# A hybrid short-convolution and Conformer decoder step: the way of the GLU output, the carried history and the convolution weights through DRAM, and the order of requests in the head

## The chip, the cores and the metric

The kernel runs on the 8 cores of one Trainium2 chip. Each core handles one prompt sequence of 2048 tokens and 16 sampling sequences of 8 new tokens each (128 sample rows), and the cores do not talk to each other. The time is the device time, in microseconds (us), of the slowest core.

## The reference, cut to what matters

```python
u = rmsnorm(h, g_mix)
a_b, a_c, a_h, a_z, b_v, b_g, b_z, gate_a, gate_b = split(u @ w_in)   # nine columns of 1024
# branch A: short gated convolution, 3 taps
s  = a_c * a_h
ya = (a_b * dwconv(concat(buf_a, s), w_conv_a) * silu(a_z)) @ w_out_a
# branch B: GLU, depthwise convolution with 31 taps, layer norm
v  = b_v * sigmoid(b_g)
ext_b = concat(buf_b, v)            # 30 carried rows (zeros for the prompt), then the new ones
c  = dwconv(ext_b, w_conv_b) + b_conv_b
yb = (silu(layernorm(c)) * silu(b_z)) @ w_out_b
new_buf_b = ext_b[:, -30:]          # sample: 22 old rows and the 8 new ones
# merge, embedding, last norm
h = h + (sigmoid(gate_a) * ya + sigmoid(gate_b) * yb) @ w_o
h = h + sigmoid(rmsnorm(h, g_ple) @ w_pg) * (p @ w_pe)
return rmsnorm(h, g_final), new_buf_a, new_buf_b
```

All matrices are 1024 wide. Inputs and weights lie in DRAM as float32; the kernel multiplies in bf16.

## The kernel before

The 2048 prompt tokens are done in two blocks of 1024; block 1 also takes the 128 sample rows (`ns = 128`, T = 1152). Each block goes through these stages, in each of which j counts eight chunks of 128 channels:

- **Head** (block 0 only, `head()`, L1029): eight tiles of x (512 KB each, issued by SyncE at L458 and L462) are squared and summed on ScalarE (`stats`, L374), the factor is made on GpSimd (L383, L388), VectorE scales (L1037), TensorE turns the tile (L1044), VectorE writes it into `uT` (L1047), and TensorE begins the first three weight columns in pieces of 128 tokens (`part`).
- **Stage B**, the loop over j at L1091: `s3_chunk(j)` (four units: h, c, z, b of branch A), `conv(j)` (the 31 taps of branch B for chunk j), `glu(j + 2)` (two units, gate and value), `wcv_load(j + 2)`. In block 1 `conv_s(j)`, the same convolution for the sample rows, is put in the middle of `glu(j + 2)`. So the GLU output of chunk j is made one whole `s3_chunk`, one `conv`, one `glu` and one more `s3_chunk` before `conv(j)` wants it.
- **Stages C and D** (L1108 to L1133): the z of branch B, the norm, output matrices of both branches, gates. **Stage E** (L1141 to L1195): 128-token tiles through w_o, w_pg and w_pe to the output, and in block 0 also the norm and the turn of block 1's x. It keeps three helpers of interest: `A_turn_dma` turns a tile by a transposing DMA, `A_turn_pe` by TensorE (tile 0 only), `palloc` gives out pairs of PSUM banks.

A **unit** (`unit_u`, L533) is one 128-column slice of weights against all T tokens: 16 matmuls of 128x512 in block 0, and 8 of 128x128 more in block 1. All are recorded at L525. Weights come from DRAM through a ring of 14 buffers: `pump` (L342) puts the next requests on GpSimd's queue, each waiting for TensorE to be done with the buffer it overwrites.

`conv(j)` needs 16 tokens by 2 channels on the partitions, so `glu_evac` (L564) sends v through DRAM. VectorE writes v into `vt[v]` as [128 channels][16 phases][W] (L570); SyncE writes it to `vd` (L597), in 2048 runs of W bf16 numbers; three loads on SyncE's queue fetch it as three 32-partition bands of `R` (L601), each waiting for that write. W is 66 in block 0 (2 + 64). In block 1 it is 114, because the sample history rides along: for each chunk `sample_hist` (L552) loads 128 x 16 x 48 float32 numbers of `sb` into columns 66 to 113 of `vt` (L555) and doubles them on GpSimd (L557), and VectorE puts the eight new rows between them (L577). `sample_hist(j + 2)` stands at the end of `glu_evac(j)`, and its multiply waits for its load on GpSimd's queue.

The weights of the convolution, `w_cv`, are 96 x 2048 float32 numbers for each chunk, of which every second one is zero: the two channels of a pair share partitions, so each has zeros where the other has its weights. `wcv_load` (L560) puts the load on GpSimd's queue.

Each engine works strictly in the order of the program (`Sched.emit`), and waits at an instruction until all its releasers have come. DMA queues of one engine are issued in that order too: at L601 SyncE waits for the write of L597, and the next chunk's L597 stands behind it. In the head `pump(2)`, `pump(1, after=["x3"])` and `pump(NRING, after=["x7"])` (L470 to L472) stand ahead of the statistics on GpSimd's queue.

Of the kernel before, what the change touches and what calls it, by code (L numbers as in the profile page):

```python
# [156 lines left out]
def build_program():  # L157
# [11 lines left out]
    sb_d = din("sb", [D, NPH, 48])  # L169
# [4 lines left out]
    w_cv = din("w_cv", [NCH, 96, 2 * D])  # L174
# [13 lines left out]
    vd = [nc.dram_tensor(f"vd{i}", [NCH, NPH, 128, b["W"]], BF16).ap() for i, b in enumerate(BLOCKS)]  # L188
    st_d = [nc.dram_tensor(f"st{i}", [2, NP + b["ns"]], F32).ap() for i, b in enumerate(BLOCKS)]

    with contextlib.ExitStack() as st:
# [53 lines left out]
        for k in range(NCH):  # L245
# [5 lines left out]

        RB = NCOL * WMAX * 2
        WR = Region("wr", 2 * RB + 2 * 4096)
        R = [WR.at(RB * i, RB // 2, BF16, [f"R{i}_{s}" for s in range(3)], group=f"R{i}") for i in range(2)]
        wcv = [WR.at(2 * RB + 4096 * i, 2 * D, BF16, [f"wcv{i}"]) for i in range(2)]
# [6 lines left out]
        u2T = [TA.at(2048 * i, D, BF16, [f"u2T{i}"]).rearrange("p (k t) -> p k t", k=NCH) for i in range(2)]  # L262
# [10 lines left out]
        VB = NPH * WMAX * 2  # L273
        XV = Region("xv", 2 * SX * 4 + 2 * VB)
        sext = [XV.at(SX * 4 * i, SX, F32, [f"sext{i}{q}" for q in ("", "l", "h", "g", "n")], group=f"sext{i}")
                for i in range(2)]
        vt = [XV.at(2 * SX * 4 + VB * i, VB // 2, BF16, [f"vt{i}{q}" for q in ("", "h", "s", "n")], group=f"vt{i}")
              for i in range(2)]
        NXS = 4
# [181 lines left out]
        for i in range(1, 8):  # L461
# [7 lines left out]
                                               scalar2=None, op0=ALU.mult), reads=["vecs"], writes=["vecs"])  # L469
        pump(2)  # L470
        pump(1, after=["x3"])
        pump(NRING, after=["x7"])  # L472
# [27 lines left out]
        def do_block(bi, blk):  # L500
            ns, W = blk["ns"], blk["W"]
# [50 lines left out]
            def sample_hist(j):  # L552
                v = j % 2
                dst = vt[v][:, 0:NPH * W].rearrange("p (h w) -> p h w", h=NPH)[:, :, 66:114]
                S.add("pool", lambda e: e.dma_start(out=dst, in_=sb_d[128 * j:128 * j + 128, :, :]),  # L555
                      writes=[f"vt{v}s", f"vt{v}n"], dma=f"vts{v}")
                S.add("pool", lambda e: e.tensor_scalar(out=dst, in0=dst, scalar1=2.0, scalar2=None, op0=ALU.mult),  # L557
                      reads=[f"vt{v}s"], writes=[f"vt{v}s"])

            def wcv_load(j):  # L560
                S.add("pool", lambda e: e.dma_start(out=wcv[j % 2][0:96, :], in_=w_cv[j, :, :]),
                      writes=[f"wcv{j % 2}"], dma=f"wcv{j % 2}")

            def glu_evac(j, bg_, bv):  # L564
# [8 lines left out]
                    reads=pres(bv) + [tgr], writes=[f"vt{v}"])  # L573
                vres = [f"vt{v}", f"vt{v}h"]
                if ns:
                    new = vv[:, 8:16, 66:114].rearrange("p t (q c) -> p t q c", c=3)[:, :, :, 2]
                    S.add("dve", lambda e: e.scalar_tensor_tensor(  # L577
                        out=new, in0=tg[:, NP:T].rearrange("p (t q) -> p t q", t=8), scalar=1.0,
                        in1=pf(bv, NP, T).rearrange("p (t q) -> p t q", t=8), op0=ALU.add, op1=ALU.mult),
                        reads=pres(bv) + [tgr, f"vt{v}s"], writes=[f"vt{v}n"])  # L580
                    vres += [f"vt{v}s", f"vt{v}n"]
# [12 lines left out]
                else:  # L594
                    S.add("act", lambda e: e.copy(out=halo_v[:, j, :, :], in_=vv[:, :, 64:66]),
                          reads=[f"vt{v}"], writes=[f"halo_v{j}"])
# [11 lines left out]
                if ns and j + 2 < NCH:  # L608
                    sample_hist(j + 2)
# [19 lines left out]
            def conv(j):  # L629
                v = j % 2  # L630
                rr = [f"R{v}_{s}" for s in range(3)] + [f"wcv{v}"]
# [88 lines left out]
            def s3_chunk(j, mid=None, mid2=None):  # L720
# [169 lines left out]
            pair_ctr = [3]  # L890
# [38 lines left out]
            def A_turn_dma(t):  # L929
                sl = t % 2  # L930
                S.add("sp", lambda e: e.dma_start_transpose(out=u2T[sl], in_=xb[sl]),
                      reads=[f"xb{sl}"], writes=[f"u2T{sl}"], dma=f"u2T{sl}")

            def A_turn_pe(t):
                sl = t % 2
                b = palloc()
                for k in range(NCH):
                    S.add("pe", lambda e, k=k: e.transpose(out=psb[:, b, k * 128:(k + 1) * 128],
                                                           in_=xb[sl][:, k * 128:(k + 1) * 128], identity=idb[:]),
                          reads=[f"xb{sl}", "idb"], writes=pr2(b))  # L940
                S.add("dve", lambda e: e.tensor_copy(out=u2T[sl], in_=psb[:, b, :].rearrange("p (k t) -> p k t", t=128)),
                      reads=pr2(b), writes=[f"u2T{sl}"])
# [205 lines left out]
            for t in range(nt):  # L1148
# [20 lines left out]
                if t > 0:  # L1169
                    D_out(t - 1)  # L1170
# [131 lines left out]
```

How the kernel before makes its waits and increments, by code:

```python
            def run(engname, e):  # L112
                waited = {}
                for o in ops:
                    if o["eng"] != engname:
                        continue
                    need = {}
                    for d in o["deps"]:
                        od = ops[d]
                        v = od["seq"] * (16 if od["dma"] is not None else 1)
                        if v > need.get(od["chan"], 0):
                            need[od["chan"]] = v
                    for c, v in need.items():
                        if waited.get(c, 0) >= v:
                            continue
                        e.wait_ge(sems[c], v)
                        waited[c] = v
                    ins = o["fn"](e)
                    if o["signal"]:
                        ins.then_inc(sems[o["chan"]], 16 if o["dma"] is not None else 1)
                if engname == final_wait_eng:
                    for c, v in final.items():
                        if waited.get(c, 0) < v:
                            e.wait_ge(sems[c], v)
```

## Time and profile before

| | |
|---|---|
| Time, median of 3 runs | 1092.92 us (1092.85 to 1106.76) |
| The profiled execution | 1104.08 us, span 1102.5 us on the slowest core |
| Spans of the 8 cores | 1078.5 to 1102.5 us |
| TensorE busy, matmuls | 848.4 us, 77% |
| VectorE, ScalarE, GpSimd busy | 468.9, 270.0 and 216.7 us |
| Stage B of block 0, first to last conv | 96.6 to 285.1 us |
| Stage B of block 1, first to last conv | 602.7 to 815.6 us |

Matmuls can overlap weight loads. An engine's busy time leaves out the instructions that issue DMAs, registers and semaphores. A row of the timeline has a start, a length, the engine (SPq is SyncE's queue), the line of the kernel, the operation, the tile written and read, and in brackets the idle time before it with what ended it.

### The profile page before, as it was taken

How to read it: one execution, taken by the hardware profiler on the slowest of the kernel's cores; microseconds unless marked ns; L12 is line 12 of the kernel's file. 1: busy time of each engine (PE TensorE's matmuls, PEld its weight loads, DVE VectorE, ACT ScalarE, POOL GpSimd, SP SyncE). 2: the span in 40 equal slices, each digit the busy share in tenths (PEclk: the TensorE clock that was granted, in tenths of full speed). 3: DMA queues.
4: the chain of work that ended last, by engine and by line, in shares of the span. 5: the costliest groups of instructions: out<-in, count | busy, mean ns of one | idle time of the engine just before them, and what ended most of it. 6: DMA issues, size and time to landing. Idle time of an engine off the chain costs nothing.

```text
span 1102.5 us, 15552 instructions; the slowest of 8 cores (1078.5 to 1102.5 us)
## 1 busy us (share of the span) xinstructions
PE 848.4 (77%) x5876; PEld 408.7 (37%) x5876; DVE 468.9 (43%) x469; ACT 270.0 (24%) x388; POOL 216.7 (20%) x362
## 2 busy tenths in 40 slices
PE   0664939598489899998851997798645989999993
PEld 0522414243234344433420543354322544454431
DVE  0511515445539322367310455364436572213554
ACT  3010202121125321356210112122102443112542
POOL 2210101011012121245213121305000222100231
PEclk9986969799789999999885999799967999999997
DMA  8598999989349675898798698999951986402632
GB/s 199 90 88 124 121 102 103 119 105 132 65 108 189 114 115 83 151 239 207 88 106 133 88 111 101 137 141 150 120 90 30 199 140 105 78 1 62 147 90 87
DMA packets 120419, 128.46 MB, mean 117 GB/s; under 512 B 80744, under 2 KB 82040, under 8 KB 118776
## 3 DMA queue, kind: packets, MB, share of 16 engines
q0 software_dynamic: 49520, 64.60, 45.6%
q1 hardware_dynamic: 70680, 62.59, 29.0%
q8 instruction: 48, 0.79, 0.3%
q14 instruction: 27, 0.22, 0.1%
q10 hardware_dynamic: 144, 0.26, 0.1%
HBM read 170.10 MB, written 17.06 MB: 170 GB/s over the span
## 4 chain that ended last, share of the span: by engine, by line
PE 41%; DMA 34%; DVE 11%; issue 7%; ACT 2%; POOL 2%; SPq 1%; DVEq 0%; POOLq 0%; ACTq 0%
PE ps L525 34%; DMA vd<-t_xv 18%; DMA t_xv<-sb 6%; PE ps L965 3%; DMA t_wr<-vd 3%; PE ps L909 2%; DMA t_wr<-w_cv 2%; DVE t_tmp L843 2%; DVE t_c L855 2%; DMA t_c<-x 1%; DVE t_tmp L991 1%; DVE t_tmp L999 1%; DMA t_wr<-w_pg 1%; PE ps L635 1%; DVE t_tmp L919 1%
## 5 line engine op out<-in xcount | busy, mean ns | idle before, releaser
L525 PE MATMUL ps<-t_uT,t_ring 128*128 128x512 bf16 (+1 forms) x2976 | 563.4, 351 | 18.1 <-DVE t_vkeep L588 12.3
L525 PEld LDWEIGHTS ps<-t_uT,t_ring 128*128 128x128 bf16 x2976 | 268.5, 100 | 305.5 <-issue 49.4
L350 POOL DMA_DIRECT2D t_ring<-w_in x144 | 77.9, 549 | 422.0 <-PE ps L525 388.7
L635 PE MATMUL ps<-t_wr 96*32 96x64 bf16 x1024 | 14.0, 218 | 139.9 <-DMA t_wr<-vd 93.3
L644 DVE STREAM_TRANSPOSE t_tmp<-ps 128x512 f32<-128x512 f32 x32 | 22.9, 715 | 139.1 <-PE ps L635 137.4
L965 PE MATMUL ps<-t_wr,t_ta 128*128 128x512 bf16 x272 | 65.9, 399 | 12.6 <-DMA t_ta<-t_acc 6.3
L525 PE MATMUL ps<-t_c,t_ring 128*128 128x512 bf16 x320 | 63.3, 350 | 9.1 <-DVE t_c L855 9.1
L616 ACT ACTIVATE t_tmp<-ps 128x1024 f32<-128x1024 f32 (+1 forms) x16 | 17.2, 1076 | 216.0 <-PE ps L525 216.0
L635 PEld LDWEIGHTS ps<-t_wr 96*32 96x32 bf16 x1024 | 11.9, 111 | 144.5 <-issue 144.1
L525 PE MATMUL ps<-t_ya,t_ring 128*128 128x512 bf16 x320 | 63.4, 354 | 0.0
L909 PE MATMUL ps<-t_wr,t_c 128*128 128x512 bf16 x272 | 61.4, 379 | 0.3 <-DVE t_c L885 0.3
L864 ACT ACTIVATE t_tmp<-ps 128x1024 f32<-128x1024 f32 (+1 forms) x32 | 34.2, 1070 | 100.4 <-PE ps L525 100.4
L869 DVE SCALAR_TENSOR_TENSOR t_ta<-t_tmp,ps 128x1024 f32<-128x1024 f32 (+1 forms) x16 | 20.6, 1288 | 87.8 <-PE ps L525 55.0
L869 DVE SCALAR_TENSOR_TENSOR t_tmp<-t_tmp,ps 128x1024 f32<-128x1024 f32 (+1 forms) x16 | 20.6, 1288 | 86.5 <-PE ps L525 79.6
L751 ACT ACTIVATE t_tmp<-ps 128x1024 f32<-128x1024 f32 (+1 forms) x16 | 17.2, 1078 | 155.3 <-PE ps L525 148.9
L781 DVE SCALAR_TENSOR_TENSOR t_tmp<-t_xv,t_vecs,t_tmp 128x1024 f32<-128x1024 f32 (+1 forms) x48 | 47.0, 980 | 4.6 <-DVE t_tmp L781 0.5
L570 DVE SCALAR_TENSOR_TENSOR t_xv<-t_tmp,ps 128x1024 bf16<-128x1024 f32 x16 | 19.5, 1221 | 68.6 <-PE ps L525 66.6
L965 PEld LDWEIGHTS ps<-t_wr,t_ta 128*128 128x128 bf16 x272 | 26.8, 102 | 50.8 <-issue 24.3
L383 POOL TENSOR_SCALAR t_msq<-t_ssq 128x1 f32<-128x1 f32 x51 | 21.9, 429 | 112.7 <-ACT t_ta L374 111.9
L525 PEld LDWEIGHTS ps<-t_c,t_ring 128*128 128x128 bf16 x320 | 28.4, 98 | 39.8 <-issue 11.7
L1008 DVE SCALAR_TENSOR_TENSOR t_tmp<-t_tmp,t_rsd,t_ya 128x1024 f32<-128x1024 f32 (+1 forms) x18 | 22.0, 1225 | 45.6 <-POOL t_rsd L388 45.6
L525 PEld LDWEIGHTS ps<-t_ya,t_ring 128*128 128x128 bf16 x320 | 29.0, 99 | 32.2 <-issue 4.3
(90 smaller groups left out, 752.9 us busy)
## 6 DMA issues: line engine op xcount, KB each, us to landing
t_ring<-w_in POOLq DMA_DIRECT2D x144, 256.0 KB, 10.6
t_xv<-x SPq DMA_DIRECT2D x26, 512.0 KB, 5.0
y<-t_tmp SPq DMA_DIRECT2D x16, 512.0 KB, 2.8
t_wr<-w_cv POOLq DMA_DIRECT2D x16, 384.0 KB, 12.9
t_c<-x SPq DMA_DIRECT2D x8, 512.0 KB, 13.1
t_ring<-w_oa POOLq DMA_DIRECT2D x16, 256.0 KB, 8.8
t_ring<-w_ob POOLq DMA_DIRECT2D x16, 256.0 KB, 4.6
t_wr<-w_o POOLq DMA_DIRECT2D x16, 256.0 KB, 12.7
```

The source lines that it names most:

```text
L350: S.add("pool", lambda e, k=k, src=src: e.dma_start(out=ring[k][:, :], in_=src), reads=after, writes=[f"ring{k}"], dma=f"ring{k}")
L525: S.add("pe", lambda e: e.matmul(psf[:, 512 * b + lo:512 * b + hi], lhsT=ring[k_][:, 128 * k:128 * k + 128], rhs=src[:, k, lo:hi], start=( ...
L635: S.add("pe", lambda e, r=r, q=q, g=g: e.matmul(psf[32 * q:32 * q + 32, 3072 + 64 * r:3072 + 64 * r + 64], lhsT=wcv[v][0:96, 32 * g:32 * g ...
L644: S.add("dve", lambda e, nb_=nb_: e.transpose(out=zv[:, nb_], in_=cp[:, :, 32 * nb_:32 * nb_ + 32].rearrange("p r (h c) -> p r h c", c=2)) ...
L781: S.add("dve", lambda e: e.scalar_tensor_tensor(out=t2[:, lo:hi], in0=src, scalar=wt[k], in1=t2[:, lo:hi], op0=ALU.mult, op1=ALU.add), rea ...
L843: S.add("dve", lambda e: e.scalar_tensor_tensor(out=tx[:, 0:T], in0=cbuf[:, j, 0:T], scalar=vcol(V_B2, j), in1=accs[:, 0:T], op0=ALU.add, ...
L855: S.add("dve", lambda e: e.tensor_tensor(out=cbufb[:, j, 0:T], in0=x[0][:, 0:T], in1=t[0][:, 0:T], op=ALU.mult), reads=[x[1], t[1]], write ...
L864: S.add("act", lambda e: e.activation(out=tg[:, 0:T], in_=pf(bg_), func=AF.Tanh, scale=0.5), reads=pres(bg_), writes=[tgr])
L869: S.add("dve", lambda e: e.scalar_tensor_tensor(out=dst[:, 0:T], in0=tg[:, 0:T], scalar=1.0, in1=pf(b), op0=ALU.add, op1=ALU.mult), reads= ...
L909: S.add("pe", lambda e, h=h, k=k: e.matmul(ps[:, b + h, :], lhsT=cbufb[:, k, TM + 128 * t:TM + 128 * t + 128], rhs=wo_t[k][:, 512 * h:512 ...
L965: S.add("pe", lambda e, h=h, k=k: e.matmul(ps[:, b + h, :], lhsT=u2T[sl][:, k, :], rhs=wpg_t[k][:, 512 * h:512 * h + 512], start=(k == 0), ...
L1008: S.add("dve", lambda e: e.scalar_tensor_tensor(out=ybuf[sl][:, lo:hi], in0=Bbuf[sl][:, lo:hi], scalar=ap, in1=gfin[:, lo:hi], op0=ALU.mul ...
```

## The change

Six things are done at once.

1. The sample history no longer passes through `vt` and `vd`. The host lays it out as `sbh`, 80 x 1024 numbers a chunk, and GpSimd's queue loads it straight into 80 partitions of a new tile `RS`; GpSimd doubles it at the start of `s3_chunk(j)`. The eight new rows go from a small tile `vn` through `vdn` into the other 16 partitions. W is 66 in both blocks.
2. The write of `vt` to `vd` is split into two halves of 8 phases, one on SyncE's queue and one on ScalarE's.
3. `w_cv` is loaded without its zeros, 96 x 1024 numbers a chunk into `wcs`, and ScalarE spreads it into `wcv` with two masked copies in `s3_chunk(j)` (`wcv_spread`).
4. In the head GpSimd's weight requests stand between the statistics of the tiles; ScalarE runs one Square and one Tanh on a dummy first.
5. The copy of 22 old rows to `hist` moves from the end of the head to before stage D of block 0, and is cut into rows of 4 KB.
6. In stage E the last tile of each block is turned by TensorE instead of the DMA, each such turn is copied out in two halves by VectorE and ScalarE, and the output of the last but one tile is made after the first half of the last.

The diff, cut:

```diff
@@ glu_evac
-                        reads=pres(bv) + [tgr, f"vt{v}s"], writes=[f"vt{v}n"])
+                        out=vn[v], in0=tg[:, NP:T], scalar=1.0, in1=pf(bv, NP, T), op0=ALU.add, op1=ALU.mult),
+                        reads=pres(bv) + [tgr], writes=[f"vn{v}"])
-                S.add("sp", lambda e: e.dma_start(out=vd[bi][j].rearrange("h p w -> p h w"), in_=vv),
-                      reads=vres, writes=[f"vd{j}"], dma=f"vd{v}")
+                for h, q in enumerate(("sp", "act")):
+                    S.add(q, lambda e, h=h: e.dma_start(out=vd[bi][j, 8 * h:8 * h + 8].rearrange("h p w -> p h w"),
+                                                        in_=vv[:, 8 * h:8 * h + 8]),
+                          reads=[f"vt{v}a", f"vt{v}h"], writes=[f"vd{j}_{h}"], dma=f"vd{v}_{h}")
+                if ns:
+                    S.add("sp", lambda e: e.dma_start(
+                        out=vdn[j].rearrange("t p q -> p t q"), in_=vn[v].rearrange("p (t q) -> p t q", t=8)),
+                        reads=[f"vn{v}"], writes=[f"vdn{j}"], dma=f"vdn{v}")
                 for s in range(3):
                     S.add("sp", lambda e, s=s: e.dma_start(
                         out=R[v][32 * s:32 * s + 32, 0:NCOL * W - s], in_=flat[:, s:NCOL * W]),
-                        reads=[f"vd{j}"], writes=[f"R{v}_{s}"], dma=f"R{v}")
+                        reads=[f"vd{j}_0", f"vd{j}_1"], writes=[f"R{v}_{s}"], dma=f"R{v}")
+                if ns:
+                    S.add("sp", lambda e: e.dma_start(
+                        out=RS[v][80:96, :], in_=vdn[j].rearrange("t (c g) q -> (t c) (g q)", c=2)),
+                        reads=[f"vdn{j}"], writes=[f"RS{v}n"], dma=f"RS{v}n")
-                if ns and j + 2 < NCH:
-                    sample_hist(j + 2)
@@ wcv_load, wcv_spread (new)
+            def wcv_load(j):
+                v = j % 2
+                S.add("pool", lambda e: e.dma_start(out=wcs[v][0:96, :], in_=w_cv[j, :, :]),
+                      writes=[f"wcs{v}"], dma=f"wcs{v}")
+                if ns:
+                    S.add("pool", lambda e: e.dma_start(out=RS[v][0:80, :], in_=sbh_d[j, :, :]),
+                          writes=[f"RS{v}h"], dma=f"RS{v}h")
+            def wcv_spread(j):
+                v = j % 2
+                for c in range(2):
+                    S.add("act", lambda e, c=c: e.activation(
+                        out=wcv[v][0:96, :].rearrange("p (m c) -> p m c", c=2)[:, :, c], in_=wcs[v][0:96, :],
+                        func=AF.Copy, scale=vecs[0:96, V_MK + c:V_MK + c + 1]),
+                        reads=[f"wcs{v}", "vecs"], writes=[f"wcv{v}_{c}"])
+                if ns:
+                    S.add("pool", lambda e: e.tensor_scalar(
+                        out=RS[v][0:80, :], in0=RS[v][0:80, :], scalar1=2.0, scalar2=None, op0=ALU.mult),
+                        reads=[f"RS{v}h"], writes=[f"RS{v}h"])
@@ s3_chunk, behind the copies that follow its first unit
+                wcv_spread(j)
                 act_flush()
@@ head
-        pump(1, after=["x3"])
-        pump(NRING, after=["x7"])
...
                         s.append(stats(t + 2))
+                        if t == 1:
+                            pump(1)
+                        if t == 3:
+                            pump(1)
+                        if t == 5:
+                            pump(NRING)
                     turn(t)
@@ stage E
-                    A_turn_dma(t + 1)
+                    if t + 2 < nt:
+                        A_turn_dma(t + 1)
...
+                elif t + 2 == nt:
+                    A_turn_pe(t + 1)
```

## Rows read from the trace of the kernel before

**Rows 1.** The page: its first line, busy time of each engine, DMA share in 40 slices.
```profile
span 1102.5 us, 15552 instructions; the slowest of 8 cores (1078.5 to 1102.5 us)
...
PE 848.4 (77%) x5876; PEld 408.7 (37%) x5876; DVE 468.9 (43%) x469; ACT 270.0 (24%) x388; POOL 216.7 (20%) x362
...
DMA  8598999989349675898798698999951986402632
```

**Rows 2.** The page, chain that ended last: share of the span by line.
```profile
PE ps L525 34%; DMA vd<-t_xv 18%; DMA t_xv<-sb 6%; PE ps L965 3%; DMA t_wr<-vd 3%; PE ps L909 2%; DMA t_wr<-w_cv 2%; DVE t_tmp L843 2%; DVE t_c L855 2%; DMA t_c<-x 1%; DVE t_tmp L991 1%; DVE t_tmp L999 1%; DMA t_wr<-w_pg 1%; PE ps L635 1%; DVE t_tmp L919 1%
```

**Rows 3.** Waits of the whole span: waiter, releaser, us in total, times, longest.
```profile
PE ps L635 <- DMA t_wr<-vd: 93.3, 5, 25.3
...
PE ps L635 <- DMA t_wr<-w_cv: 46.6, 3, 26.8
...
POOL t_xv L557 <- DMA t_xv<-sb: 95.2, 8, 17.3
```

**Rows 4.** Timeline of the head: start us, us, engine, line, operation [idle before <-releaser].
```profile
6.77 1.06 ACT L374 ACTIVATE t_ta<-t_c 128x1024 bf16<-128x1024 f32 x1
...
22.02 5.80 POOL L350 DMA_DIRECT2D t_ring<-w_in  x11 [5.29 <-DMA t_c<-x]
...
28.89 0.75 DVE L1037 TENSOR_SCALAR t_acc<-t_c,t_rsd 128x1024 bf16<-128x1024 f32 x1 [23.02 <-POOL t_rsd L388]
...
49.85 0.75 DVE L1037 TENSOR_SCALAR t_acc<-t_c,t_rsd 128x1024 bf16<-128x1024 f32 x1
...
55.09 1.22 DVE L570 SCALAR_TENSOR_TENSOR t_xv<-t_tmp,ps 128x1024 bf16<-128x1024 f32 x1 [1.98 <-ACT t_xv L568]
```

**Rows 5.** Timeline of TensorE, stage B of block 0.
```profile
96.56 1.04 PE L635 MATMUL ps<-t_wr 96*32 96x64 bf16 x64 [23.26 <-DMA t_wr<-vd]
...
97.53 23.39 PE L525 MATMUL ps<-t_uT,t_ring 128*128 128x512 bf16 x96
...
121.54 20.88 PE L525 MATMUL ps<-t_uT,t_ring 128*128 128x512 bf16 x96
...
159.68 1.04 PE L635 MATMUL ps<-t_wr 96*32 96x64 bf16 x64 [17.26 <-DMA t_wr<-vd]
...
285.07 1.04 PE L635 MATMUL ps<-t_wr 96*32 96x64 bf16 x64 [14.82 <-DMA t_wr<-vd]
```

**Rows 6.** Timeline of block 0, queues of SyncE and GpSimd around two GLU writes.
```profile
89.87 0.38 SPq L597 DMA_DIRECT2D vd<-t_xv  x1
...
102.67 1.23 SPq L601 DMA_DIRECT2D t_wr<-vd  x3
...
103.94 0.76 SPq L1082 DMA_DIRECT2D hist<-sbn  x1
...
104.26 0.53 POOL L350 DMA_DIRECT2D t_ring<-w_in  x1 [29.83 <-PE ps L525]
...
108.65 0.38 SPq L597 DMA_DIRECT2D vd<-t_xv  x1
...
150.22 1.24 SPq L601 DMA_DIRECT2D t_wr<-vd  x3
```

**Rows 7.** Timeline of TensorE, stage B of block 1.
```profile
543.70 9.25 PE L525 MATMUL ps<-t_uT,t_ring 128*128 128x512 bf16 x48 [3.94 <-DVE t_vkeep L588]
...
602.66 1.05 PE L635 MATMUL ps<-t_wr 96*32 96x64 bf16 x64 [26.77 <-DMA t_wr<-w_cv]
...
610.28 19.67 PE L525 MATMUL ps<-t_uT,t_ring 128*128 128x512 bf16 x120
...
815.60 1.04 PE L635 MATMUL ps<-t_wr 96*32 96x64 bf16 x64 [25.32 <-DMA t_wr<-vd]
```

**Rows 8.** DMA issues of the w_cv load: count, KB each, median us to landing.
```profile
t_wr<-w_cv POOLq DMA_DIRECT2D x16, 384.0 KB, 12.9
```

**Rows 9.** Groups by line and shape: busy us, mean ns | idle before <-releasers.
```profile
L496 ACT ACTIVATE t_wr<-t_wr,t_vecs 128x1024 bf16<-128x1024 bf16 x16 | 18.3, 1143 | 55.5 <-DMA t_wr<-w_pg 55.5
```

**Rows 10.** Timeline of the last tile, TensorE.
```profile
1082.68 5.07 PE L965 MATMUL ps<-t_wr,t_ta 128*128 128x512 bf16 x16 [2.75 <-DMA t_ta<-t_acc]
```

More of the change, by code:

```diff
@@ L173, in build_program @@
     w_ob = din("w_ob", [NCH, 128, D])
-    w_cv = din("w_cv", [NCH, 96, 2 * D])
+    w_cv = din("w_cv", [NCH, 96, D])
     w_o = din("w_o", [D, D])
@@ L261, in build_program @@
         tas = [TA.at(TM * 4 * i, TM, F32, [f"ta{i}"]) for i in range(2)]
[L262 removed]
+        u2T = [TA.at(2048 * i, D, BF16, [f"u2T{i}_0", f"u2T{i}_1"], group=f"u2T{i}").rearrange("p (k t) -> p k t", k=NCH) for i in range(2)]
         junk = TA.at(4096, D, BF16, ["junk"])
@@ L630, in conv @@
                 v = j % 2
-                rr = [f"R{v}_{s}" for s in range(3)] + [f"wcv{v}"]
+                rr = [f"R{v}_{s}" for s in range(3)] + [f"wcv{v}_0", f"wcv{v}_1"]
                 for r in range(16):
@@ L657, in conv_s @@
                 v = j % 2
-                rr = [f"R{v}_{s}" for s in range(3)] + [f"wcv{v}"]
+                rr = [f"RS{v}h", f"RS{v}n", f"wcv{v}_0", f"wcv{v}_1"]
                 for r in range(16):
@@ L937, in A_turn_pe @@
                 for k in range(NCH):
[L938 to L942, printed above, removed]
+                    S.add("pe", lambda e, k=k: e.transpose(
+                        out=psb[:, b + k // 4, (k % 4) * 128:(k % 4) * 128 + 128],
+                        in_=xb[sl][:, k * 128:(k + 1) * 128], identity=idb[:]),
+                          reads=[f"xb{sl}", "idb"], writes=[f"ps{b + k // 4}"])
+                src = [psb[:, b + i, 0:512].rearrange("p (k t) -> p k t", t=128) for i in range(2)]
+                S.add("dve", lambda e: e.tensor_copy(out=u2T[sl][:, 0:4], in_=src[0]),
+                      reads=[f"ps{b}"], writes=[f"u2T{sl}_0"])
+                S.add("act", lambda e: e.copy(out=u2T[sl][:, 4:8], in_=src[1]),
+                      reads=[f"ps{b + 1}"], writes=[f"u2T{sl}_1"])
             def A_sq(t):
@@ L1081, in do_block @@
                 head()
-                S.add("sp", lambda e: e.dma_start(out=hist_d, in_=sbn_d[:, 8 * D:30 * D]), dma="hist")
                 S.add("sp", lambda e: e.dma_start(out=hista[:], in_=sa_d), writes=["hista"], dma="hista")
             else:
-                for j in range(2):
-                    sample_hist(j)
                 glu(0)
@@ L1123, in do_block @@
             xload(min(xst["nd"] + NXS, xst["cap"]))
+            if not last:
+                S.add("sp", lambda e: e.dma_start(
+                    out=hist_d.rearrange("s (h d) -> s h d", d=D),
+                    in_=sbn_d.rearrange("s (h d) -> s h d", d=D)[:, 8:30, :]), dma="hist")
             for j in range(NCH):
@@ L1168, in do_block @@
                     n_turn(n)
-                if t > 0:
+                if t > 0 and not (last and t == nt - 1):
                     D_out(t - 1)
@@ L1235 @@
                 if 0 <= d < 31:
-                    for c in range(2):
-                        cv[:, s, pi, c, :, po, c] = wcb[30 - d, :, :, c]
-    cv = cv.reshape(NCH, 96, 2 * D)
+                    cv[:, s, pi, :, :, po] = wcb[30 - d].transpose(0, 2, 1)
+    cv = cv.reshape(NCH, 96, D)
+    vecs[:, V_MK] = np.arange(128) % 2 == 0
+    vecs[:, V_MK + 1] = np.arange(128) % 2 == 1
     def tiled(w):
```

84 lines of the change are left out of this document (43 added, 41 removed).

## The prediction

> **What bounds the kernel now.** I began with the page. TensorE's matmuls are busy for 848 us of 1102, so 254 us of the span hold none, and no other engine comes near that [rows 1]. The chain that ended last gives a third of the span to unit matmuls, but 18% to the write of `vd`, 6% to the load of `sb`, and 3% and 2% to the loads of `R` and `w_cv` [rows 2]. The waits say who is kept: `conv` (L635) waits 93.3 us for `R` in 5 places and 46.6 us for `w_cv` in 3, and GpSimd stands 95.2 us at the doubling of the history, with the weight requests behind it on its queue [rows 3]. The timelines give the places. In the head, x7 has come at 22.0 us, yet the first scale starts at 28.9 because GpSimd waits for x7 to request weights first [rows 4]. In block 0 every second `conv` finds no `R` [rows 5], with one of 12.7 us like these between them. In block 1 TensorE stops before the first `conv` and again later [rows 7]. So it is bound by TensorE plus stops in stage B, and the stops are latencies of a DRAM round trip.
>
> Why is the round trip slow? The second `vd` write of block 0 is issued at 89.9 and its first reader at 102.7: under 13 us. In that stretch GpSimd had requested no weight for 29.8 us. The third is issued at 108.7 and lands at 150.2, 41 us for the same bytes, with weights, `w_cv` and, ahead of it on its own queue, the `hist` copy [rows 6]. What makes it slow is what runs beside it.
>
> **The change part by part.** All against the profiled execution, 1104.1 us (span 1102.5 and 1.6 around it). That is 1.0% over the median of 1092.9; the result is scaled by 0.990 at the end.
>
> *a) Head and first conv.* Now: first scale 28.9, last scale 49.9, so 3.0 us a tile over seven steps, and the evacuation of the first GLU 5.2 us later, at 55.1 [rows 4]. With the requests behind the statistics, the first square ends at 7.8 [rows 4], the scale follows 1 to 2 us later, say at 9.5; seven steps of 3.0 give 30.5, and 5.2 more is 35.7. The last x bounds it from the other side: 22.0 plus a square and the factor, some 2 us, plus 5.2 is 29. I take 36, 19 us earlier. The third weight column is asked for later relative to TensorE's work, worth up to 3 us, hidden in rounding up. The dummy activations take a table load off a stretch where ScalarE only waited for x0; nothing counted.
> The first `conv` is at 96.6 after 23.3 of idle [rows 5], so TensorE needs 96.6 - 23.3 - 55.1 = 18.2 us of work from that evacuation, and could be there at 54. It will not be: 10 weights are requested only behind x7, at about 23, and `vd`, `R` and the first `wcs` compete with them. If the write still takes from 55.1 to the SyncE row at 89.9 [rows 4, 6], about 33 us, `conv` comes at 36 + 33 + 8 = 77; if it takes half, at 61, but then `wcs(0)`, queued behind some 15 weights, is last, and two copies of 1.1 us [rows 9] stand behind it. I take 70: gain 26.5, bounds 18 and 42.
>
> *b) Stage B, block 0.* From 96.6 to 285.1 are 188.5 us. The work in it is 38 units of 20.88 / 6 = 3.48 us and seven convs of 0.7: 137 us [rows 5]. So 51 us is excess: three stops (44.8 us) and slow matmuls after each (23.4 us for the six units that take 20.9 otherwise). A write in two halves on two queues should have twice the turns beside the weight queue. 34 us of pure competition (41 less some 7 of `hist`, priced below) become 17; with `R` 9 us (150.2 to 159.7) [rows 5, 6] the trip is 27 us, against 36 us of TensorE work between `glu(j)` and `conv(j)` (10 units, one conv). The stop should vanish; what is late next is the `w_cv` load, 12.9 us to landing [rows 8], now wanted a chunk start (14 us) earlier but requested 22 us ahead and half as large. SyncE's queue also becomes shorter: a waiting L601 holds the next write for 17 us and not 41. The two spreading copies cost ScalarE 16 x 2 x 1.14 = 37 us over the kernel [rows 9]; ScalarE is busy 24%, and they stand between two evacuations that are a unit or two apart (3.5 us), so nothing on the path, but up to 2.3 us for each chunk where `wcs` is late, since the evacuations behind are held too. ScalarE's own half write waits for VectorE's evacuation; behind it on ScalarE is the copy of the next unit, 3.5 us away: nothing. Moving `hist` off the queue is worth its time there, some 7 us of one of the stops (bounds 0 and 15), and is within the sum. I leave 15 us of stops: gain 36, bounds 5 and 51.
>
> Here a rule of the Trainium skill speaks against it. The trace shows 13 us with an idle weight queue and 41 with a busy one [rows 6], but no write on two queues. "DMA: Bandwidth & Descriptors", section "Issuing engines are not separate DMA queues", says that starting DMAs on several engines saves only the sequencer's time for starting them, as all run on the same 16 DMA engines. The same page ("Queues, rings and completion order") has each DMA engine take turns between the queues that have work, and by that the second queue gets turns from the weights. By the one the sum is that of rival 1, by the other the one above; the halving itself is my estimate from the 13 and 41 us.
>
> *c) Tail of block 0:* the last turn by TensorE for a DMA; 2 us (0 and 3).
>
> *d) Block 1 up to its first conv.* From 543.7 to 602.7 are 59.0 us, for 5 units (120 matmuls) that take 19.7 at full pace; with the 3.9 us before, 43 us are lost [rows 7]. All of it hangs on `sb`: VectorE's L577 waits for GpSimd's doubling, `vd` waits for both, and `w_cv` is requested only behind four loads and doublings. This goes. The new load of 80 rows and its doubling stay on GpSimd's queue, but behind `wcs` and only twice in this place; 14 weights are in the ring to cover that. What is late next is `wcs(0)` and `RS`, requested behind the fourth unit, with 4 units (16 us) until `conv` against 12.9 us [rows 8] and two copies: I leave 5. Gain 38, bounds 25 and 43.
>
> *e) Stage B, block 1.* 602.7 to 815.6 are 213 us; the work is 38 units of 3.93 and some 10 us of convs, 159 [rows 7]; excess 54. Two of the stops are for `w_cv`, behind the history on GpSimd; the last, 25.3, is a `vd` write beside weights. The write shrinks from 114 to 66 numbers in each run, at an unchanged number of runs; `vdn` adds 1024 short runs on SyncE, ahead of the loads of `R` (under 2 us, since 2048 went in 13). I leave 15. Gain 39, bounds 20 and 54.
>
> *f) Tail.* The last matmuls wait 2.75 us for a transposing DMA [rows 10], and one 1.3 us product leaves the last chain: 3 us (0 and 5).
>
> Sum: 26.5 + 36 + 2 + 38 + 39 + 3 = 144.5, so 959.6, by 0.990 is **950 us**. The lower bounds sum to 68 (1026), the upper to 198 (897).
>
> **Rivals.**
> 1. *The second queue gives nothing*; the turns are not what limits the short runs. For: nothing in the trace shows two such queues. Against: the 13 and 41 us [rows 6] hang on what runs beside. Then a) gains 18, b) only `hist`, 8, e) loses the last stop and gains 26: 18 + 8 + 2 + 38 + 26 + 3 = 95, 1009, scaled **999**.
> 2. *The DMA engines are full.* Their share is 8 or 9 tenths in each of the eight slices over stage B of block 0 and in most over that of block 1 [rows 1]. If the stops only let the DMAs catch up, stage B shortens by the removed traffic: half of `w_cv` and `hist`, about 7% of 189 us, 13; in block 1 also the `sb` loads and the wider `vd` and `R`, 28: 22 + 13 + 2 + 38 + 28 + 3 = 106, scaled **988**. Against: in the stop before 96.6 the weight queue ran dry (GpSimd's 29.8 us), and no unit waits long for a weight.
> 3. *Slower: ScalarE as the gate.* The spread waits for `wcs` in order, and the evacuation of z behind it holds TensorE's banks. To lose the 144.5 us and 21 more it must cost about 12 us in each of 14 chunks, so `wcs` would have to land 12 + 8 (two units) + 22 = 42 us after its request. The load lands after 12.9 us in the middle [rows 8]. If it did: 1104 + 23, scaled **1115**.
> 4. *The change lets all of it through but gains little* (later weights in the head, history still late): within 2%, about **1080**.
>
> **How the numbers follow.** Forecast 0.60, rival 1 0.17, rival 2 0.15, rival 4 0.05, rival 3 0.03. Faster by over 2% (less than 1071, about the least that can be told from no change here): 0.92; within 2% 0.05; slower 0.03. The forecast's own spread is 905 to 985; the range must reach rivals 1 and 2 and leaves out the extremes of either side and rivals 3 and 4: 912 to 1022.
>
> **What would show it.** `vd` writes from two queues land in about 17 us beside weights (rival 1: 30 and more). The first GLU evacuation is at 36 us, the first `conv` at 70 and in block 1 about 20 us after its fourth unit. L635's waits fall from 140 us to 45 or less; GpSimd's wait at L557 is gone. TensorE's share rises from 77% to 88%. If units wait for the ring instead, it is rival 2; if ScalarE waits for `wcs` and TensorE for ScalarE, rival 3. The prediction fails most easily in b), if the round trip stays above 36 us.

## The result

The changed kernel takes 1046.9 us (median of 4 runs, 1044.1 to 1051.4) where the kernel before took 1098.9 in the same comparison: a ratio of 0.948, interval 0.937 to 0.959. That is 52 us faster. The prediction said 950, with a range of 912 to 1022; the result lies above it. Some executions of either kernel are longer by a few per cent, with a lower granted clock on one die (the profiled one of the changed kernel is among them, though its 1044.1 us lies between the 1039.0 and 1046.8 of undisturbed ones); ratios here and below leave them out, medians do not, so a ratio can be lower than that of the medians.

The first line of the page, the busy times and the DMA share, as in [rows 1]:

```profile
span 1042.5 us, 15748 instructions; the slowest of 8 cores (1002.1 to 1042.5 us)
...
PE 856.6 (82%) x5892; PEld 412.4 (40%) x5892; DVE 481.0 (46%) x471; ACT 314.5 (30%) x426; POOL 218.5 (21%) x362
...
DMA  9999998997289875799498999999927965204531
```

TensorE is busy for 82% of the span, not 88%, and the DMA share still stands at 8 or 9 tenths in nearly every slice of both stages B. The chain by line, as [rows 2]:

```profile
PE ps L534 39%; DMA vd<-t_xv 16%; DMA t_wr<-vd 4%; PE ps L991 3%; PE ps L931 3%; DMA t_c<-x 2%; DMA t_wr<-w_pg 2%; DVE t_tmp L865 2%; DVE t_c L877 2%; ACT t_ta L381 1%; DVE t_tmp L1017 1%; DVE t_tmp L803 1%; DVE t_tmp L800 1%; DVE t_tmp L941 1%; DVE t_tmp L1025 1%
```

The write of `vd` still has 16% of it; the load of `sb` is gone. The waits, against [rows 3] (L656 is `conv`, L572 the spreading copies, L773 and L790 the evacuations of z and b in `s3_chunk`):

```profile
PE ps L656 <- DMA t_wr<-vd: 75.7, 6, 21.2
...
ACT t_wr L572 <- DMA t_wr<-w_cv: 28.7, 2, 14.4
...
DVE t_tmp L790 <- ACT t_tmp L773: 28.7, 2, 14.5
```

`conv` waits 75.7 us for `R`, down from 93.3, and no longer for the weights; GpSimd's 95 us at the history are gone but for one wait of 15.4 us, for the new load of `sbh`. ScalarE stands 28.7 us for `wcs` twice, and VectorE behind it for as long, but at the first chunk of each block, where TensorE waits for `R` anyway. The head, as the last of [rows 4] (L1063 is the scale, L587 the evacuation):

```profile
33.19 0.75 DVE L1063 TENSOR_SCALAR t_acc<-t_c,t_rsd 128x1024 bf16<-128x1024 f32 x1 [1.45 <-POOL t_rsd L395]
...
38.88 1.22 DVE L587 SCALAR_TENSOR_TENSOR t_xv<-t_tmp,ps 128x1024 bf16<-128x1024 f32 x1 [2.39 <-ACT t_xv L585]
```

The first GLU output is evacuated at 38.9 us instead of 55.1. TensorE in stage B of block 0, as [rows 5]:

```profile
78.44 1.05 PE L656 MATMUL ps<-t_wr 96*32 96x64 bf16 x64 [21.15 <-DMA t_wr<-vd]
...
102.34 20.88 PE L534 MATMUL ps<-t_uT,t_ring 128*128 128x512 bf16 x96
...
164.68 1.04 PE L656 MATMUL ps<-t_wr 96*32 96x64 bf16 x64 [19.96 <-DMA t_wr<-vd]
...
258.28 1.04 PE L656 MATMUL ps<-t_wr 96*32 96x64 bf16 x64 [6.83 <-DMA t_wr<-vd]
```

and of block 1, as [rows 7] (L684 is `conv_s`):

```profile
558.73 1.05 PE L656 MATMUL ps<-t_wr 96*32 96x64 bf16 x64 [17.99 <-DMA t_wr<-vd]
...
593.19 0.19 PE L684 MATMUL ps<-t_wr 96*32 96x32 bf16 x2 [2.02 <-issue]
...
738.60 0.62 PE L656 MATMUL ps<-t_wr 96*32 96x64 bf16 x31 [4.81 <-issue]
...
750.47 0.70 PE L656 MATMUL ps<-t_wr 96*32 96x64 bf16 x64
```

Some stops went, others stayed. Two rows are of another kind: TensorE stops inside `conv` or `conv_s` and waits for nothing that the profile shows ("issue"). In stage B of block 1 there are five, 16 us in all; the trace of before has one such stop, of 1.9 us, inside a unit. And the fourth GLU write of block 0 with the one behind it, as [rows 6] (L611 the write, L620 the loads of `R`):

```profile
110.96 0.38 SPq L611 DMA_DIRECT2D vd<-t_xv  x1
149.31 1.32 SPq L620 DMA_DIRECT2D t_wr<-vd  x3
150.78 0.46 SPq L611 DMA_DIRECT2D vd<-t_xv  x1
170.50 1.23 SPq L620 DMA_DIRECT2D t_wr<-vd  x3
```

That is 38 us from the issue to the landing of both halves with two queues, and 20 for the next. The median by kind of DMA (count, KB each, us from issue to landing), with [rows 8]:

```profile
t_ring<-w_in POOLq DMA_DIRECT2D x144, 256.0 KB, 13.0
...
t_wr<-w_cv POOLq DMA_DIRECT2D x16, 192.0 KB, 16.4
vd<-t_xv SPq DMA_DIRECT2D x16, 132.0 KB, 19.3
```

Everything that runs in stage B lands late: a weight column takes 13.0 us where it took 10.6, a half write 19.3, `w_cv` at half its size 16.4 where it took 12.9. Between the two profiled executions the 60 us came from these places:

| stretch | before | after | gained | predicted |
|---|---|---|---|---|
| to the first conv (a) | 96.6 | 78.4 | 18.1 | 26.5 |
| stage B, block 0 (b) | 188.5 | 179.8 | 8.7 | 36 |
| to the first conv of block 1 (c, d) | 317.6 | 300.5 | 17.1 | 40 |
| stage B, block 1 (e) | 212.9 | 191.7 | 21.2 | 39 |
| to the end (f) | 286.9 | 292.0 | -5.1 | 3 |

### The profile page after: what moved, and what is told of

It is laid out like the page before. It is cut to its first block, busy times and chain, and to the rows that moved or that the text cites. A ratio compares the mean times of both kernels' runs of the same rounds, so it can differ in the third digit from the quotient of the medians.

```text
span 1042.5 us, 15748 instructions; the slowest of 8 cores (1002.1 to 1042.5 us)
## 1 busy us (share of the span) xinstructions
PE 856.6 (82%) x5892; PEld 412.4 (40%) x5892; DVE 481.0 (46%) x471; ACT 314.5 (30%) x426; POOL 218.5 (21%) x362
## 3 DMA queue, kind: packets, MB, share of 16 engines
q1 hardware_dynamic: 60760, 54.14, 26.5%
## 4 chain that ended last, share of the span: by engine, by line
PE 47%; DMA 26%; DVE 13%; issue 8%; ACT 3%; SPq 1%; POOL 1%; DVEq 0%; POOLq 0%; ACTq 0%
PE ps L534 39%; DMA vd<-t_xv 16%; DMA t_wr<-vd 4%; PE ps L991 3%; PE ps L931 3%; DMA t_c<-x 2%; DMA t_wr<-w_pg 2%; DVE t_tmp L865 2%; DVE t_c L877 2%; ACT t_ta L381 1%; DVE t_tmp L1017 1%; DVE t_tmp L803 1%; DVE t_tmp L800 1%; DVE t_tmp L941 1%; DVE t_tmp L1025 1%
## 5 line engine op out<-in xcount | busy, mean ns | idle before, releaser
L656 PE MATMUL ps<-t_wr 96*32 96x64 bf16 x1024 | 13.9, 213 | 83.8 <-DMA t_wr<-vd 75.7
L886 ACT ACTIVATE t_tmp<-ps 128x1024 f32<-128x1024 f32 (+1 forms) x32 | 34.2, 1070 | 99.4 <-PE ps L534 99.4
L637 ACT ACTIVATE t_tmp<-ps 128x1024 f32<-128x1024 f32 (+1 forms) x16 | 17.2, 1076 | 126.9 <-PE ps L534 126.6
L587 DVE SCALAR_TENSOR_TENSOR t_xv<-t_tmp,ps 128x1024 bf16<-128x1024 f32 x16 | 19.5, 1221 | 72.0 <-PE ps L534 69.6
L572 ACT ACTIVATE t_wr<-t_wr,t_vecs 96x1024 bf16<-96x1024 bf16 x32 | 43.7, 1432 | 28.7 <-DMA t_wr<-w_cv 28.7
L390 POOL TENSOR_SCALAR t_msq<-t_ssq 128x1 f32<-128x1 f32 x51 | 24.0, 471 | 131.4 <-ACT t_ta L381 131.1
L747 ACT COPY t_tmp<-ps 128x1024 f32<-128x1024 f32 (+1 forms) x16 | 17.1, 1067 | 102.8 <-PE ps L534 102.8
L656 PEld LDWEIGHTS ps<-t_wr 96*32 96x32 bf16 x1024 | 11.6, 108 | 88.5 <-issue 87.9
L790 DVE TENSOR_TENSOR t_tmp<-ps,t_tmp 128x1024 f32<-128x1024 f32 (+1 forms) x16 | 20.7, 1291 | 56.0 <-ACT t_tmp L773 28.7
```

Of the source, the lines that this page charges most:

```text
L390: S.add("pool", lambda e, c=c, add=add: e.tensor_scalar(out=msq[:, c:c + 1], in0=ssq[:, c:c + 1], scalar1=f / D, scalar2=add, op0=ALU.mult ...
L572: S.add("act", lambda e, c=c: e.activation(out=wcv[v][0:96, :].rearrange("p (m c) -> p m c", c=2)[:, :, c], in_=wcs[v][0:96, :], func=AF.C ...
L656: S.add("pe", lambda e, r=r, q=q, g=g: e.matmul(psf[32 * q:32 * q + 32, 3072 + 64 * r:3072 + 64 * r + 64], lhsT=wcv[v][0:96, 32 * g:32 * g ...
L886: S.add("act", lambda e: e.activation(out=tg[:, 0:T], in_=pf(bg_), func=AF.Tanh, scale=0.5), reads=pres(bg_), writes=[tgr])
```

## The experiments

Each ratio is to the kernel before on the same chip. The four runs under 1 ran together, and so did the four under 2. The first three under 3 ran beside the first of the versions with short reads; the shifted runs beside the kernel before with long runs, the second version with short reads and the one with all bands read in short runs; two more of 4 (short reads a third time, aligned runs from two queues) together on yet another chip. A comparison across such groups is one of ratios and is good to about 1%: the changed kernel had 0.948 and 0.945, the undivided write 0.934 and 0.942. "The undivided write" is the changed kernel with part 2 undone.

**1. One part undone.** Is it the second queue, the spreading copies, the order in the head or the place of `hist`?

```diff
-                for h, q in enumerate(("sp", "act")):      # two halves
+                S.add("sp", ... out=vd[bi][j].rearrange("h p w -> p h w"), in_=vv)
```

> The changed kernel (1046.9 us) with the GLU write undivided on SyncE's queue again. Theory A, the DMA engines are what is full and a second queue only changes who waits: within 8 us of 1047, writes land in 25 to 40 us beside weights as in the changed kernel. Rival B, the second queue does what was predicted and the gain went elsewhere: 25 us or more slower, 1072 and up, with the waits of conv back near 95 us.

Measured 1014.3, ratio 0.934 (0.928 to 0.940): faster than with two queues, so rival B falls. Theory A had no gain at all and landings of 25 to 40 us, and its numbers fail too. The whole write lands in 18.7 us, where each half of the divided one took 19.3: halving it had saved nothing. Weights and `w_cv` land sooner in this profile, though a second one of the same kernel has 12.0 us for a weight column:

```profile
t_ring<-w_in POOLq DMA_DIRECT2D x144, 256.0 KB, 10.9
...
vd<-t_xv SPq DMA_DIRECT2D x16, 264.0 KB, 18.7
...
t_wr<-w_cv POOLq DMA_DIRECT2D x16, 192.0 KB, 12.6
```

```diff
-    w_cv = din("w_cv", [NCH, 96, D])            # wcs, two masked copies
+    w_cv = din("w_cv", [NCH, 96, 2 * D])        # straight into wcv, no copies
```

> The changed kernel with the convolution weights loaded with their zeros and no spreading copies. Theory A (DMA engines full): the 3 MB landed more come back as 10 to 20 us, 1057 to 1067. Rival C, the two copies on ScalarE behind a wait are a new stop that eats the gain: the same or faster, 1035 to 1047.

Measured 1039.2, ratio 0.955 (0.947 to 0.963), about 1% from the changed kernel's 0.948 and 0.945, with intervals that overlap. Rival C's gain does not show, and theory A's loss of 10 to 20 us is at the edge of what can be told.

```diff
         pump(2)
+        pump(1, after=["x3"])
+        pump(NRING, after=["x7"])
-    (the three pumps between the statistics)
```

> The changed kernel with the weight requests of the head ahead of the statistics again. If the 18 us by which the first conv came earlier are kept to the end: 1065. Theory A says that part of them is lost to fuller DMA engines in the stage behind: 1052 to 1062.

Measured 1042.2, ratio 0.957 (0.949 to 0.965). The first conv is 21 us later (99.2 against 78.4), the last conv of block 0 only 11 (269.6 against 258.3), and the whole some 1% slower, with intervals that overlap. So in the profile half of what the head wins is lost by the end of stage B, as theory A said; the total alone could not tell.

```diff
-            if not last:      # hist, ahead of stage D
+            if last:
```

> The changed kernel with the copy of the 22 old rows moved once more, to before stage D of block 1 (the same instruction, block 1 for block 0). If its place in block 0 is why w_pg came late and TensorE stood 4.5 us and ran slower behind it: 4 to 8 us faster, about 1041. If not: 1047 as now.

It took 1055.9 us in the middle, from 1026 to 1083, too wide for a ratio. In its profile the stretch from the last conv of block 0 to the first of block 1 is 295.2 us, in the changed kernel's of the next group 294.1: nothing gained. The place of `hist` is not why w_pg comes late.

**2. Queue or runs?**

> The changed kernel as it is, as a yardstick on the same chip as the three runs beside it: a ratio to the kernel before of 0.94 to 0.96, as measured first.

The ratio is 0.945 (0.939 to 0.952).

```diff
-                for h, q in enumerate(("sp", "act")):
+                for h, q in enumerate(("sp", "sp")):
```

> The changed kernel with both halves of the GLU write on SyncE's queue. Undoing the split altogether gave a ratio of 0.934 where the changed kernel had 0.948. Theory D, it is the second queue that costs (its short runs get turns from the weights and the reads of R): as the undivided write, 20 to 30 us faster than the changed kernel beside it. Rival E, it is the cut in two instructions that costs: no faster than the changed kernel.

The ratio is 0.940 (0.930 to 0.950), between the two; neither theory is settled by it.

> The changed kernel with the whole GLU write on ScalarE's queue, the loads of R on SyncE's. Theory D (what costs is that short runs take two turns of three beside the weights): like one queue, 15 to 30 us faster than the changed kernel, since a write then has one turn beside the weights. Rival F, ScalarE's own queue or its waits cost: as slow as the changed kernel or slower.

The ratio is 0.947 (0.940 to 0.955), with TensorE standing 8.0 and 10.9 us for a copy of ScalarE at the first chunks: no better than two queues. Of the four ways to issue the write none is faster than the plain one; the differences are 1.4% at most.

```diff
-   out=vd[bi][j].rearrange("h p w -> p h w")                                # 2048 runs of 132 bytes
+   out=vd[bi][j].rearrange("h p w -> (h p w)").rearrange("(p h w) -> p h w", p=128, h=NPH)   # 128 of 2112
```

> The changed kernel with the whole write on SyncE's queue and the GLU output laid down as 128 runs of 2112 bytes instead of 2048 of 132; the loads of R read the same bytes of DRAM, so the values that reach the convolution are in the wrong places. Theory A, the short runs are what fills the DMA engines and makes the trip long: writes land within 6 us even beside weights, the waits of conv all but vanish, and 30 to 50 us are won on the undivided write. Rival G, the trip waits for the weights and DRAM traffic whatever its shape: within 10 us of the undivided write, landing in 15 us and more.

It took 931.6 us, ratio 0.853 (0.848 to 0.859). The same bytes and the same waits, and it takes some 90 us less than the undivided write, where theory A had 30 to 50. `conv` waits for `R` nowhere in it, and the two stages B last 137.5 and 159.5 us. The landings:

```profile
t_ring<-w_in POOLq DMA_DIRECT2D x144, 256.0 KB, 5.4
...
vd<-t_xv SPq DMA_DIRECT2D x16, 264.0 KB, 5.1
...
t_wr<-w_cv POOLq DMA_DIRECT2D x16, 192.0 KB, 5.7
```

The write lands in 5.1 us and not 18.7, and the weight columns beside it land in 5.4 us, where the profiles with short runs so far have 10.4 to 13.0. The 2048 short runs slow what runs beside them. TensorE gains twice, for its stops are gone and its granted clock is higher: the mean over stage B of block 0 is 0.87 in the kernel before, 0.90 in the changed one and 1.00 here.

**3. What in the runs?** A run is called crooked here when it begins or ends off a multiple of 64 bytes, counted from the start of `vd`, and straight otherwise. Of the 132-byte runs every one is crooked; the long runs of 2112 bytes are straight as well as long, so the two have to be told apart. The 64 only sorts the layouts tried; which multiple counts was not measured.

> The changed kernel with the GLU write undivided on SyncE's queue, a second time, as the yardstick for the three beside it: a ratio of 0.934 to the kernel before if the first measurement holds, 0.945 if its gain over the changed kernel was luck.

The ratio is 0.942 (0.936 to 0.949). With the 0.934 of the first time the undivided write is 0.3 to 1.4% better than the change; no more can be said.

```diff
+   out=...rearrange("(a p b) -> p a b", p=128, a=8)      # 1024 runs of 264 bytes
```

> As the undivided write, but the same bytes are laid down in 1024 runs of 264 bytes instead of 2048 of 132 (values reach the convolution in the wrong places). Theory A1, each run written to DRAM has a price of its own: half of the way to the long runs, a ratio of 0.89 to 0.90. Theory A2, what costs is that a run is short or crooked at all: more than three quarters of the loss stays, 0.92 and up.

It took 950.2 us, ratio 0.875 (0.871 to 0.879): three quarters of the gain for half the runs, more than A1 allows and far from A2. Its weight columns land in 8.2 us, about half way between 5.4 and the 10.9 and 12.0 of the undivided write, so a price for each crooked run is not excluded by it; what excludes a price for each run as such is the next one.

```diff
-    vd ... [NCH, NPH, 128, W]
+    vd ... [NCH, NPH, 128, NCOL]
-   out=vd[bi][j].rearrange("h p w -> p h w"), in_=vv
+   out=vd[bi][j].rearrange("h p w -> p h w"), in_=vv[:, :, 2:66]      # 2048 runs of 128 bytes
```

> As the undivided write, but 2048 runs of 128 bytes, each beginning on a multiple of 128, without the two halo numbers (their products are missing from the convolution, and the three bands are equal). Theory A1, each run has its price: as the undivided write, 0.934. Theory A3, the price is of runs that begin and end inside a line of DRAM: near the long runs, 0.855 to 0.875.

It took 950.1 us, ratio 0.866 (0.862 to 0.871): as many runs as ever, and almost as fast as the long ones. The landings:

```profile
t_ring<-w_in POOLq DMA_DIRECT2D x144, 256.0 KB, 5.2
...
vd<-t_xv SPq DMA_DIRECT2D x16, 256.0 KB, 7.2
```

So A3 holds, and A1 falls. But the length and the halo had changed too, so:

```diff
-    vd ... [NCH, NPH, 128, NCOL]
+    vd ... [NCH, NPH * 128 * NCOL + 64], begun at element 2      # the same runs, 4 bytes further
```

> The kernel with 2048 aligned runs of 128 bytes (0.866), all of them moved by 4 bytes in DRAM: same count, same length, same neighbours. If what costs is a run that begins and ends inside a line of DRAM: back to 0.93 to 0.945, the undivided write's. If it was the length of 132 bytes or the missing halo: 0.866 again.

It took 1084.8 us in the middle (1066.9 to 1110.4), too wide for a ratio, but its lowest run is 128 us above the lowest of the aligned ones (938.6), and above every run of the changed kernel. Landings and TensorE's waits (L654 `conv`, L682 `conv_s`; us in total, times, longest):

```profile
t_ring<-w_in POOLq DMA_DIRECT2D x144, 256.0 KB, 12.2
...
t_wr<-w_cv POOLq DMA_DIRECT2D x16, 192.0 KB, 12.9
```

```profile
PE ps L654 <- DMA t_wr<-vd: 73.7, 9, 20.7
...
PE ps L682 <- issue: 18.0, 9, 7.0
```

Four bytes of offset are the whole difference between 12.2 and 5.2 us for a weight column, with the same number and length of runs. The loss is larger than forecast: the 132-byte runs cost less than these of 128, and why is open. The stops without a releaser are back too, 18 us in `conv_s` alone; in the profiles with long or aligned runs there are none over 1.5 us. A rival is left: in the crooked layouts neighbouring runs, which come from neighbouring partitions, also meet inside one multiple of 64 bytes. Crooked runs with a gap between them were not tried, so an unfilled line and a line shared by two writers are not told apart.

**4. Where was the loss, and can it be avoided?**

> The kernel before with its GLU output laid down in long runs (2112 and 3648 bytes; values reach the convolution in the wrong places). If crooked runs were the main loss before the change too: 60 to 90 us faster than before, 0.92 to 0.945, and the rest of the way to the changed kernel with long runs (0.853) is what the other parts of the change are worth once DMA time is free. If the waits of the kernel before were mainly its own (history, head): 0.97 and up.

It took 965.3 us, ratio 0.886 (0.882 to 0.890): more than expected. The kernel before lost 124 us (0.114 of 1090.9) to the shape of its runs, more than twice what the whole change won. The one long stop that is left before a `conv` is its own, the wait for `w_cv` behind the history:

```profile
518.07 1.05 PE L635 MATMUL ps<-t_wr 96*32 96x64 bf16 x64 [16.67 <-DMA t_wr<-w_cv]
```

Against long runs in the changed kernel (0.853, with the write undivided) the other parts of the change are worth a factor of 0.963, some 35 us, on straight runs: they work.

```diff
+   out=vd[bi][j], in_=vv                                  # vd is [128][16][66]: 128 runs of 2112 bytes
+   for c in range(2):                                     # band 0, in 132-byte reads
+       out=R[v][c:32:2, 0:NCOL * W].rearrange("h (g w) -> h g w", w=W),
+       in_=vd[bi][j, 64 * c:64 * c + 64].rearrange("g h w -> h g w")
+   for s in range(1, 3):                                  # bands 1 and 2, SBUF to SBUF
+       out=R[v][32 * s:32 * s + 32, 0:NCOL * W - s], in_=R[v][0:32, s:NCOL * W]
```

> A version that may beat both kernels, with the reference's full result: v goes to DRAM as 128 runs of 2112 bytes, the first band of R is read in 2048 runs of 132 bytes, and the other two bands are copied from the first inside SBUF in long rows. If short runs cost when they are written to DRAM and little when they are read: 0.86 to 0.89 (the trip has one more step, about 8 us, within the 36 us that it has). If a short run costs the same on either side: 0.93 and up.

> The version with long writes and short reads once more, for its ratio: 0.865 to 0.885 to the kernel before.

> The version with long writes and short reads a third time, since its ratio was not settled: 0.865 to 0.885.

The first two spread too widely for a ratio (955.8 and 976.1 in the middle, lowest 938.6 and 957.0); the third gave 0.863 (0.860 to 0.866), 952.6 in the middle, from 935.9 to 1031.2, with 1083.6 the lowest of the kernel before beside it. It computes the whole reference and beats both kernels, by 14% and, by the ratios, by some 9%. Page and landings of the third:

```profile
span 941.4 us, 15688 instructions; the slowest of 8 cores (926.2 to 941.4 us)
...
PE 827.4 (88%) x5798; PEld 405.3 (43%) x5892; DVE 480.2 (51%) x471; ACT 314.5 (33%) x426; POOL 221.3 (24%) x362
```

```profile
t_ring<-w_in POOLq DMA_DIRECT2D x144, 256.0 KB, 5.0
...
vd<-t_xv SPq DMA_DIRECT2D x16, 264.0 KB, 5.4
t_wr<-vd SPq DMA_DIRECT2D x32, 132.0 KB, 6.1
t_wr<-t_wr SPq DMA_DIRECT2D x16, 263.9 KB, 4.4
```

> As short_reads, but all three bands are read from DRAM in runs of 132, 130 and 128 bytes (6144 short reads a chunk) and none is copied in SBUF. If short reads are cheap: within 1% of short_reads. If a short run costs a DMA engine much on the reading side too: 20 us slower or more, with the share of conv's waits back.

The ratio is 0.875 (0.871 to 0.879), 958.3 us in the middle: a little over 1% from the version above, on another chip, so between the two forecasts. Three times as many crooked reads, with the copies inside SBUF gone, cost about 1 point of the ratio, where 2048 crooked writes cost 8 or 9 (0.934 and 0.942 against 0.853).

> The aligned runs of 128 bytes, written from two queues as in the change (halo left out as there). With one queue they gave 0.866. If the second queue is worth nothing once the runs are straight: 0.86 to 0.875. If it was worth what the prediction said and crooked runs hid it: below 0.855.

It took 953.9 us, ratio 0.866 (0.860 to 0.872), against 0.866 (0.862 to 0.871) with one queue: on straight runs the second queue is worth nothing that these runs can tell.

## Why the prediction was wrong

**The step that failed is b), "a write in two halves on two queues should have twice the turns beside the weight queue", and with it the price that e) and a) took from it.** I read 13 us with an idle weight queue and 41 with a busy one [rows 6] as turns, and halved it. The measured half writes took 19.3 us in the middle and up to 38.2. The 19.3 looks near the 17 that I forecast, but that is luck: the undivided write takes 18.7, so the halving gave nothing. What the two rows show is a collision that slows both sides, and the weights' side was there to be seen as well, in landings of 10.6 us for a weight column (5.4 in the changed kernel with long runs). I priced the write and left its neighbours at their durations. The rule that I weighed against the change, from the Trainium skill ("DMA: Bandwidth & Descriptors", section "Issuing engines are not separate DMA queues"), is the one that the runs bear out: 0.866 with one queue and with two on straight runs, and on crooked ones 0.945 and 0.948 with two against 0.934 and 0.942 with one.

**a)** 26.5 predicted, 18.1 measured. The evacuation came at 38.9 and not 36: ScalarE had x7 only at 30.8 and no longer at 22.0, with the third and fourth weight columns now requested while x was still coming, so the last scale was at 33.2 (with the old order put back it had x7 at 22.1); then `conv` waited 21 us for `R` because the first write took 29. With long runs the first conv stands at 57.2: the latency was mis-sized, the reordering was right.

**b)** 36 predicted, 8.7 measured; four stops, 36.6 us in all, where I left 15. The work in the stage, 137 us, was right to the microsecond: with long runs the stage lasts 137.5. (In the rows of before the convs that wait are the first, third, fifth and eighth, not quite "every second"; nothing in the sum hangs on it.)

**c)** 2 predicted, 8.3 lost. Block 1's first unit begins 18.5 us earlier than before (509.4 and 527.9) although the last conv of block 0 is 26.8 earlier. Part of it is this stop, where ScalarE stood for the w_pg load and TensorE for ScalarE:

```profile
352.29 5.13 PE L534 MATMUL ps<-t_ya,t_ring 128*128 128x512 bf16 x16 [4.51 <-ACT t_tmp L886]
```

It is there with `hist` moved (1.9 us) and with long runs (6.9 us) as well. Its weights are asked for when stage B ends, and that is earlier now; why it costs more than before stays open.

**d)** 38 predicted, 25.4 measured, from block 1's first unit to its first conv. The history did leave the path: TensorE never waits for it. Yet a stop of 18.0 us stands before the first conv where I left 5, now for `R` and not for `w_cv` [rows 7]: again the write.

**e)** 39 predicted, 21.2 measured. The waits of `conv` in the stage are gone; in their place came the stops without a releaser, 16 us, which no rival named, and slower matmuls behind them (22.5 us at most for the five units that take 19.7). With long runs the stage lasts 159.5 us, and I had put its work at 159. The price of `vdn` was wrong by my own sum: 1024 runs, when 2048 went in 13 us, are 6.5 us and not under 2. It landed in 25.0 us in the middle (5.6 with long runs), and once, at the start of the block, in 36.7, with SyncE standing for it until 556.3 us; no stop of TensorE followed from that one.

**f)** 3 predicted, -5.1 measured. Of that, 3.8 us were lost before the first matmul of stage E, 0.6 in stage E up to the last tile's product, and 0.8 from there to the end. The last turn by TensorE takes away a wait for a DMA and meets one for VectorE, 3.6 us for 2.75:

```profile
1021.90 6.52 PE L991 MATMUL ps<-t_wr,t_ta 128*128 128x512 bf16 x16 [3.63 <-DVE t_tmp L1017]
```

This does not hang on the runs: with long runs in both, the stretch is 289.2 us in the changed kernel and 284.8 in the kernel before. Why stages C and D take longer is open.

**The spreading copies** cost 1432 ns each and not 1143:

```profile
L572 ACT ACTIVATE t_wr<-t_wr,t_vecs 96x1024 bf16<-96x1024 bf16 x32 | 43.7, 1432 | 28.7 <-DMA t_wr<-w_cv 28.7
```

They stayed off the path, as said, and rival 3 did not come about: it is the first chunk of each block alone that waits. Rival 1 (999) had the mechanism of the queue right, and rival 2 (988) that DMA time is short; both were priced as if what remains kept its pace, and so both came out too fast, by 48 and 59 us.

**What would have shown it.** That a run costs by where it begins could not be read from the trace of before. But the page of before has a share of 8 or 9 tenths at 88 to 132 GB/s in stage B of block 0, beside 199 GB/s in the first slice, and that says that the DMA engines are full of something other than bytes. I took the share for a rival and gave it 0.15. The share alone would not have done: in the kernel before it is 0.91 and 0.89 in the two stages B, at 114 and 123 GB/s; with long runs it is still 0.88 and 0.91, at 157 and 160 GB/s, and the stops inside both stages are gone but for one of 0.6 us.

## What to carry to other kernels

Look at where each run of a DRAM write begins and ends before anything else about a DMA: a halo of two numbers made 64 into 66 and took every run off its multiple of 128 bytes, and that cost the kernel before 124 us, where the order of requests, the size of loads and the layout of weights together were worth some 35. When transfers land late, compare the landings of their neighbours too; if both are slow, a second queue shares the trouble and does not halve it. If a rearrangement must be made of short runs, make them on the reading side.

## What the runs showed of the hardware

With all 8 cores at work, runs of 128 bytes written to DRAM on multiples of 128 cost little against runs of 2112 (0.866 and 0.853), the same runs 4 bytes off cost over 100 us in a kernel of 950, and short reads little (0.863 and 0.875). The Trainium skill ("DMA: Bandwidth & Descriptors", section "Specifications") puts the limit at 512 bytes, below which a transfer is read, changed and written back. Here 128 aligned bytes did well and 132 or 264 crooked ones did not, so the measurement puts the weight on alignment rather than on length. The 32-byte runs of `vdn`, 1024 for each chunk of block 1 and each beginning on a multiple of 32, are also in the changed kernel with long runs, where stage B of block 1 takes no more than its work, 159.5 us: runs so short, and this few, cost nothing that shows there. Whether it is DRAM or the DMA engine that does the extra work was not tried, nor whether one core alone would see it.

TensorE's stops with no releaser, most of them inside a row of small matmuls, come with the crooked runs (16 us in the changed kernel, 18 in `conv_s` of the shifted one, none over 1.5 us in the long and the aligned ones). How many there are varies among kernels with the same runs: the kernel before has one, of 1.9 us. What TensorE waits for in them is not shown.
